# A norm's factor applied behind the matmul, with the shift as two further columns, in the last up stage of a float32 network

## The chip, the cores and the metric

The kernel runs on one core of a Trainium2 chip. The metric is the device time of one execution in microseconds (us). Durations of single instructions are in us too, unless ns is written. TensorE (PE) has two levels of clock, 1.2 and 2.4 GHz; the profile gives the granted clock as a share of the higher one.

## The reference, cut to what matters

A network on 256 tokens of width 1024, all in float32: a short-convolution layer, a latent-attention layer, and then one block of a second model with gated linear attention (GLA) and a squared-relu MLP. The change is in the MLP of that last block:

```
def modulate(h, shift, scale):
    return h * (1 + scale) + shift
def sqrelu_mlp(h, w1, w2):
    return jnp.square(jax.nn.relu(h @ w1)) @ w2
h_lat = h_lat + mod_l[2] * o_lat
h_lat = h_lat + mod_l[5] * sqrelu_mlp(modulate(rmsnorm(h_lat, norm2_g[i]), mod_l[3], mod_l[4]),
                                      mlp_w1[i], mlp_w2[i])
return rmsnorm(h_lat, final_g)
```

rmsnorm divides each token by the root of the mean of its squares and multiplies by a gain. w1 is 1024 x 4096, w2 is 4096 x 1024. The vectors mod_l (scale, shift, gates) are products of a condition with a large matrix (here "ada").

## The kernel before, in words

Activations lie feature-major: a tile of 128 partitions holds 128 features, and its T = 256 columns are the tokens. h holds the 8 chunks (DC) of the stream. A matmul multiplies a 128 x 128 block of weights with such a chunk; every product is made of three float32r matmuls, hi x hi, lo x hi and hi x lo, where hi is the value in float32r and lo the rest, so that the result has float32's precision.

The weights come as one stream of units: a unit is 128 x 1024, eight blocks, 24 matmuls. SyncE loads each position of the stream into a ring of four slots (raw). ScalarE makes whi by a copy (hi(), line 745), VectorE makes wlo by a subtraction (lo(), line 1154) and so frees the slot. TensorE starts a unit when its wlo is done (slot_of_next_unit). Both splits run three units ahead of TensorE (LEAD = 3); hi() of a unit waits until TensorE has finished the unit four before. Now and then a position holds a piece of the ada matrix instead; VectorE multiplies it with the condition (ada_dot, line 1236). Each engine has a program of its own, written out by hand in the order in which it runs; an engine waits at a semaphore, and everything behind that wait in its program waits too. Class Counts keeps the semaphores' counts: take waits for one more, sig raises, again waits for all counted so far.

The last block's end, for all engines:

- gla_out (8 units, inside resid(1, None, gate=2 * DC) on VectorE and resid(1, None) on ScalarE): when a unit's result is there, VectorE adds it, times the gate, to h (line 1322), ScalarE squares h (line 754), VectorE adds the square to ssum (line 1172) and makes the next wlo.
- The norm: TensorE's stat() sums ssum over the partitions (line 454, one plain float32 matmul that the trace shows as two), ScalarE takes the root (line 760), VectorE the reciprocal (line 1181, rstd). modulated then makes for each of the 8 chunks a32 = h x gmod x rstd on VectorE (line 1514), xhi = a32 + shift on ScalarE (line 930), and xlo on VectorE (line 1518).
- mlp_up, MC = 32 units, one result tile of 4096 features' 128 each: units(MC, DC, xhi, xlo, chunks=x_ready). The first two units are done together, chunk by chunk, as the chunks come (lines 390 to 392), the others one after the other (lines 408 to 410). For result j ScalarE makes mr = relu(result) (line 1121), VectorE ms = mr x mr (line 1689), ScalarE mhi of chunk j-1 (inner_hi, line 1116), VectorE mlo of chunk j-1 (inner_lo, line 1684) and then the next wlo. Chunks go in cycles of four: chunk 0 of a cycle has no inner part; at chunk 3 the inner part is done for 2 and for 3, and an ada product stands at the end. It is a loop of two times sixteen chunks.
- mlp_down, 8 results of four units each, which TensorE starts when 31 of the 32 mlo are there; then the last norm and the store.

The two up stages of the earlier layers (ffn_up) already have the norm's factor on the result: line 1260 multiplies the result by rstd on VectorE, line 785 is the step of ScalarE that follows.

Of the kernel before, what the change touches and what calls it, by code (L numbers as in the profile page):

```python
# [23 lines left out]
P = 128  # L24
T = 256
# [130 lines left out]
def at(t, k):  # L156

    return t[:, k * T:(k + 1) * T] if isinstance(k, int) else t[:, bass.ds(k * T, T)]


def program(nc, stream, xT, ctxT, vec, cst, rot, wa2, crow, out):
    ctx = ExitStack()

    def sb(name, cols, dt=F32, stack=ctx, rows=P):
        return stack.enter_context(nc.sbuf_tensor(name, [rows, cols], dt))

    with ctx:
# [96 lines left out]
        stage = ExitStack()  # L264
        mhi = sb("mhi", MC * T, F32R, stage)
        mlo = sb("mlo", MC * T, F32R, stage)
        mr = sb("mr", 4 * T, F32, stage)
        ms = sb("ms", 4 * T, F32, stage)
        stage.close()
        ps = [ctx.enter_context(nc.psum_tensor(f"ps{i}", [P, 512], F32)) for i in range(8)]  # L270
        STAT = ps[4]
# [40 lines left out]
        def cst_of(name):  # L312
            return ct[:, CST[name][0]:CST[name][0] + CST[name][1]]
# [2 lines left out]
            return rt_tab[:, ROT[name][0]:ROT[name][0] + ROT[name][1]]  # L316

        ones, ident = cst_of("ones"), cst_of("ident")
        ada_junk, cr_ctx = state[:, 0:D], state[:, D:2 * D]
        block = ctx.enter_context(nc.Block())  # L320

# [35 lines left out]
        def _(pe):  # L357
# [15 lines left out]
                c.n["unit"] = u + 1  # L373
                return u % RING

            def units(n, K, hi, lo, sizes=(BLK,), lag=RING, chunks=None, then=None, after=0, final=None):

                blk, begin = 0, 0  # L380
                if chunks is not None and then is None:
                    pair = [slot_of_next_unit() for _ in range(2)]
                    for j in range(2):
                        tile_free(tile[0] + j, lag)
                    for k in range(K):
                        c.take(chunks)
                        for j, slot in enumerate(pair):
                            dst = ps[(tile[0] + j) % lag][:, 0:T]
                            w = slice(slot * D + k * P, slot * D + (k + 1) * P)
                            pe.matmul(dst, whi[:, w], at(hi, k), start=(k == 0), stop=False)  # L390
                            pe.matmul(dst, whi[:, w], at(lo, k), start=False, stop=False)
                            last = pe.matmul(dst, wlo[:, w], at(hi, k), start=False, stop=(k == K - 1))
                            if k == K - 1:
                                c.sig(last, pe_units)
                    blk, begin = 2 * K, 2
                for j in range(begin, n):
                    slot = slot_of_next_unit()
                    for b in range(sizes[j % len(sizes)]):
                        t, k = tile[0] + blk // K, blk % K
                        if k == 0:  # L400
                            tile_free(t, lag)
                        dst = ps[t % lag][:, 0:T]
                        w = slice(slot * D + b * P, slot * D + (b + 1) * P)
                        if chunks is not None and j == 0 and begin == 0:
                            c.take(chunks)
                        if final is not None and k == K - 1:
                            pe.wait_ge(y_ready, final)
                        pe.matmul(dst, whi[:, w], at(hi, k), start=(k == 0), stop=False)  # L408
                        pe.matmul(dst, whi[:, w], at(lo, k), start=False, stop=False)  # L409
                        last = pe.matmul(dst, wlo[:, w], at(hi, k), start=False, stop=(k == K - 1))  # L410
                        blk += 1
                    c.sig(last, pe_units)
                    if then is not None and j == after:
                        then()
                tile[0] += blk // K
# [41 lines left out]
            def stat():  # L457
                c.take(ssum_ready, 8)
                stat_of([ssum[:, 0:T]])
# [250 lines left out]
            gla_stat(3)  # L710
            gla_out_chunks(4, DC)
            units(DC - 2, DC, zhi, zlo)
            stat()
            units(MC, DC, xhi, xlo, chunks=x_ready)
            c.take(y_ready, MC - 1)
            c.n["y_ready"] += 1
            looped(DC // 2, 8, MC, mhi, mlo, lag=2, final=c.n["y_ready"])
# [3 lines left out]
        def _(act):  # L721
            c = Counts(act)

            def settled():


                act.wait_ge(ev("tables"), 32)
# [70 lines left out]
            def resid(units_per, gain, gained=None, beside_ctx=False):  # L798


                per = {hi_ready: 4 * units_per, tile_read: 4, sq_ready: 8 if gained else 4}
                if gain:
                    per[xhi_ready] = 4
                if beside_ctx:
                    per |= {ev("zc_raw"): 4, ev("zc_hi"): 4}
                with c.loop(2, per) as i:
                    for m in range(4):
                        hi(units_per)
                        if beside_ctx:
                            settled()  # L810
                            c.take(ev("zc_raw"))
                            c.sig(act.activation(at(zhi, i * 4 + m), at(c32, i * 4 + m), ACT.Identity,
                                                 bias=mod[:, bass.ds(i * 4 + (6 * DC + m), 1)]), ev("zc_hi"))
                        settled()
                        c.take(tile_read)
                        if gain:
                            c.sig(act.activation(at(xhi, i * 4 + m), at(h, i * 4 + m), ACT.Copy,
                                                 scale=vt[:, bass.ds(i * 4 + (VEC[gain][0] + m), 1)]), xhi_ready)
                        square(h, i * 4 + m, 0 if gained else m)
                        if gained:  # L820
                            square(h, i * 4 + m, 1, vt_col(i * 4 + (VEC[gained][0] + m)))
# [105 lines left out]
            def modulated(dst, s0, units_after=()):  # L927
                for k in range(DC):
                    c.take(a_ready)
                    c.sig(act.activation(at(dst, k), at(a32, k), ACT.Identity, bias=mod[:, s0 + k:s0 + k + 1]), xhi_ready)  # L930
                    if k in units_after:
                        hi()
# [172 lines left out]
            head_hi(2)  # L1105
            head_root()
            head_hi(3)
            resid(1, None)
            sqrt_stat(D)
            modulated(xhi, 3 * DC)  # L1110
            c.n["pe_units"] = UNITS - 2 * MC
            with c.loop(2, {hi_ready: 16, pe_units: 16, tile_read: 16, y_f32: 16, yhi_ready: 16}) as i:
                def inner_hi(j):
                    settled()
                    c.take(y_f32)
                    c.sig(act.activation(at(mhi, i * 16 + j), at(ms, j % 4), ACT.Copy), yhi_ready)

                for j in range(16):
                    hi()
                    c.take(pe_units)  # L1120
                    c.sig(act.activation(at(mr, j % 4), ps[j % 4][:, 0:T], ACT.Relu), tile_read)
                    if j % 4:
                        inner_hi(j - 1)
                    if j % 4 == 3:
                        inner_hi(j)
# [13 lines left out]
        def _(dve):  # L1139
# [39 lines left out]
            def reciprocal_root(dst):  # L1179
                c.take(root_ready)  # L1180
                c.sig(dve.reciprocal(dst[:, :], root[:, :]), rstd_ready)  # L1181
                c.again(rstd_ready)
# [491 lines left out]
                head_norm(hd)  # L1674
            c.again(slots_done)
            mod_of(2 * DC, 5 * DC, 1, 4 * DC, "g_n2")
            resid(1, None, gate=2 * DC)
            reciprocal_root(rstd)
            modulated(h, DC, 3 * DC, xlo)
            with c.loop(2, {hi_ready: 16, "unit": 16, slots_done: 20, tile_read: 16, y_f32: 16, yhi_ready: 16,  # L1680
                            y_ready: 16}) as i:
                def inner_lo(j):
                    c.take(yhi_ready)
                    c.sig(dve.tensor_tensor(at(mlo, i * 16 + j), at(ms, j % 4), at(mhi, i * 16 + j), ALU.subtract),  # L1684
                          y_ready)

                for j in range(16):
                    c.take(tile_read)
                    c.sig(dve.tensor_tensor(at(ms, j % 4), at(mr, j % 4), at(mr, j % 4), ALU.mult), y_f32)
                    if j % 4:  # L1690
                        inner_lo(j - 1)
                    lo()
                    if j % 4 == 3:
                        inner_lo(j)
                        ada_dot(5 * DC + j // 4, i * 4 + (5 * DC + j // 4))
            c.again(slots_done)
            mod_of(5 * DC, 6 * DC, 0, 0, None)
            c.n["pe_units"] += MC
            clear_sum()

            def mlp_down(first):
# [132 lines left out]
```

## Time and profile before

| | us |
|---|---|
| median of 3 runs | 1019.96 |
| lowest and highest | 1016.63, 1024.02 |
| the profiled execution, its own time | 1022.39 |
| span of its profile | 1020.5 |
| granted clock of TensorE, mean | 0.986 |

The span runs from the first to the last instruction on the core. A timeline's or a chain's row gives the start, the duration, the engine (PEld is TensorE's weight load, an engine with q its sequencer), the line of the kernel, what is written and read, the count, and in brackets how long the engine stood idle before and who released it. ps is a result in PSUM.

### The profile page before, as it was taken

What the parts mean: (1) busy time and instruction counts of PE and PEld (TensorE: products, weight loads), DVE (VectorE), ACT (ScalarE), POOL (GpSimd) and SP (SyncE); (2) the same over time, 40 slices, a digit from 0 to 9 for tenths busy, and PEclk for the clock granted to TensorE, in tenths of its full rate; (3) what the DMA queues carried; (4) which work ended last, traced back from release to release, by engine and by line L of the source; (5) the groups of instructions that cost most, each with busy time, mean ns of one, the idle gap of its engine ahead of it and who ended that gap; (6) DMA issues with size and microseconds to landing.
All of it is one profiled execution on the core that took longest, in us unless ns stands there. A gap on an engine that the chain in (4) does not pass through costs nothing.

```text
span 1020.5 us, 21669 instructions
## 1 busy us (share of the span) xinstructions
PE 953.1 (93%) x7410; PEld 925.3 (91%) x7410; DVE 811.5 (80%) x1347; ACT 551.2 (54%) x876; POOL 1.2 (0%) x6
## 2 busy tenths in 40 slices
PE   4999999999999987999999997989999879999996
PEld 4999999999999877999999996878898879999995
DVE  5998899998889888899998887877536787775553
ACT  6545666665546435666666555766433456563331
POOL 0000000000000000000000000000000000000000
PEclk9999999999999999999999998999999989999998
DMA  8677565556786543555555884786530337766541
GB/s 328 216 247 242 167 203 185 185 185 198 271 267 223 173 148 103 177 195 191 184 185 177 288 263 141 240 287 209 185 103 22 124 121 243 235 226 207 184 165 41
DMA packets 54452, 197.32 MB, mean 193 GB/s; under 512 B 6046, under 2 KB 7198, under 8 KB 54144
## 3 DMA queue, kind: packets, MB, share of 16 engines
q1 hardware_dynamic: 54256, 195.55, 57.8%
q10 hardware_dynamic: 144, 1.05, 0.3%
q8 instruction: 36, 0.59, 0.2%
q14 instruction: 16, 0.13, 0.0%
HBM read 195.53 MB, written 1.05 MB: 193 GB/s over the span
## 4 chain that ended last, share of the span: by engine, by line
PE 80%; DVE 11%; ACT 3%; DMA 3%; issue 2%; DVEq 0%; SPq 0%; ACTq 0%
PE ps L408 23%; PE ps L410 23%; PE ps L409 23%; DVE wlo L1154 3%; DMA raw<-stream 2%; DVE raw L1236 1%; ACT whi L745 1%; PE ps L454 1%; PE ps L438 1%; DVE rstd L1181 1%; PE ps L440 1%; PE ps L439 1%; PE ps L574 1%; PE ps L590 1%; DMA ct<-cst 1%
## 5 line engine op out<-in xcount | busy, mean ns | idle before, releaser
L1154 DVE TENSOR_TENSOR wlo<-raw,whi 128x1024 fp32r<-128x1024 f32 x306 | 371.4, 1219 | 84.8 <-ACT whi L745 84.1
L745 ACT ACTIVATE whi<-raw 128x1024 fp32r<-128x1024 f32 x306 | 321.1, 1052 | 126.1 <-PE ps L410 60.2
L408 PE MATMUL ps<-xhi,whi 128*128 128x256 f32 x1288 | 366.3, 284 | 18.2 <-DVE wlo L1154 15.7
L409 PE MATMUL ps<-xlo,whi 128*128 128x256 f32 x1288 | 363.4, 282 | 0.0
L410 PE MATMUL ps<-xhi,wlo 128*128 128x256 f32 x1288 | 363.3, 282 | 0.0
L408 PEld LDWEIGHTS ps<-xhi,whi 128*128 128x128 f32 x1288 | 244.9, 190 | 19.7 <-issue 14.9
L409 PEld LDWEIGHTS ps<-xlo,whi 128*128 128x128 f32 x1288 | 245.0, 190 | 0.7 <-issue 0.5
L410 PEld LDWEIGHTS ps<-xhi,wlo 128*128 128x128 f32 x1288 | 245.0, 190 | 0.0
L408 PE MATMUL ps<-yhi,whi 128*128 128x256 f32 x400 | 112.5, 281 | 3.0 <-DVE ylo L1252 3.0
L409 PE MATMUL ps<-ylo,whi 128*128 128x256 f32 x400 | 112.3, 281 | 0.0
L410 PE MATMUL ps<-yhi,wlo 128*128 128x256 f32 x400 | 112.3, 281 | 0.0
L785 ACT ACTIVATE cv<-U,vt 128x256 f32<-128x256 f32 x88 | 44.9, 510 | 86.6 <-DVE U L1260 86.6
L408 PEld LDWEIGHTS ps<-yhi,whi 128*128 128x128 f32 x400 | 75.4, 189 | 3.4 <-issue 3.4
L409 PEld LDWEIGHTS ps<-ylo,whi 128*128 128x128 f32 x400 | 75.5, 189 | 0.0
L410 PEld LDWEIGHTS ps<-yhi,wlo 128*128 128x128 f32 x400 | 75.5, 189 | 0.0
L408 PE MATMUL ps<-mhi,whi 128*128 128x256 f32 x256 | 72.1, 282 | 2.5 <-DVE mlo L1684 1.6
L410 PE MATMUL ps<-mhi,wlo 128*128 128x256 f32 x256 | 71.9, 281 | 0.0
L409 PE MATMUL ps<-mlo,whi 128*128 128x256 f32 x256 | 71.9, 281 | 0.0
L1236 DVE SCALAR_TENSOR_TENSOR raw<-raw,cr 128x1024 f32<-128x1024 f32 x48 | 58.4, 1218 | 0.0
L408 PEld LDWEIGHTS ps<-mhi,whi 128*128 128x128 f32 x256 | 48.3, 189 | 2.9 <-issue 1.8
L409 PEld LDWEIGHTS ps<-mlo,whi 128*128 128x128 f32 x256 | 48.3, 189 | 0.0
L410 PEld LDWEIGHTS ps<-mhi,wlo 128*128 128x128 f32 x256 | 48.3, 189 | 0.0
(272 smaller groups left out, 1450.8 us busy)
## 6 DMA issues: line engine op xcount, KB each, us to landing
raw<-stream SPq DMA_DIRECT2D x362, 512.0 KB, 3.6
h<-xT SPq DMA_DIRECT2D x1, 1024.0 KB, 4.7
c<-ctxT ACTq DMA_DIRECT2D x1, 1024.0 KB, 7.1
out<-h SPq DMA_DIRECT2D x8, 128.0 KB, 2.1
ct<-cst SPq DMA_DIRECT2D x1, 962.5 KB, 6.8
rt_tab<-rot SPq DMA_DIRECT2D x1, 960.0 KB
cr<-crow SPq DMA_DIRECT2D x1, 512.0 KB, 10.6
state<-crow SPq DMA_DIRECT2D x1, 512.0 KB, 11.5
```

The source lines that it names most:

```text
L408: pe.matmul(dst, whi[:, w], at(hi, k), start=(k == 0), stop=False)
L409: pe.matmul(dst, whi[:, w], at(lo, k), start=False, stop=False)
L410: last = pe.matmul(dst, wlo[:, w], at(hi, k), start=False, stop=(k == K - 1))
L438: pe.matmul(dst, hi[:, tok], whi[:, w], start=first, stop=False)
L439: pe.matmul(dst, lo[:, tok], whi[:, w], start=False, stop=False)
L440: last = pe.matmul(dst, hi[:, tok], wlo[:, w], start=False, stop=final)
L454: last = pe.matmul(STAT[:, 0:width], ones, piece, start=(k == 0), stop=(k == len(pieces) - 1))
L574: pe.matmul(ps[5 + n % 3][:, b * T:(b + 1) * T], gates, sums[:, b * P:(b + 2) * P], start=True, stop=True)
L745: c.sig(act.activation(whi[:, s * D:(s + 1) * D], raw[:, r * D:(r + 1) * D], ACT.Copy), hi_ready)
L785: c.sig(act.activation(at(cv, j), U[:, j * (T + 2) + 2:(j + 1) * (T + 2)], ACT.Copy, scale=vt_col(i * 12 + (base + 3 * j + 2))), tap_ready)
L1154: c.sig(dve.tensor_tensor(wlo[:, w], raw[:, r], whi[:, w], ALU.subtract), slots_done)
L1236: c.sig(dve.scalar_tensor_tensor(out=tile_w, in0=tile_w, scalar=1.0, in1=cr[:, :], op0=ALU.mult, op1=ALU.mult, accum_out=into(t)), slots_done)
```

## The change

The normalised input of the last up stage is no longer made. In its place nhi and nlo hold h x gmod (no factor of the token), with chunks of T + 2 columns; the two further columns of each chunk hold the shift. As the factor is the same for all features of a token it is applied behind the matmul: each result, now 258 wide, is multiplied on VectorE by rstd2, which is rstd in 256 columns and 1 in the last two. So columns 0 to 255 hold the scaled part, and column 256 the shift's share, a number for each feature, which ScalarE's relu takes as its bias. ScalarE then squares too. The statistic stands behind the first unit of the stage (then=stat) and not ahead of it; TensorE waits for shift_ready before the stage. On ScalarE nhi is made inside the loop of gla_out, on VectorE nlo.

```diff
+def at2(t, k):
+    return t[:, k * (T + 2):(k + 1) * (T + 2)]
...
+        shift_twice = mod[:, 3 * DC:4 * DC].unsqueeze(2).to_broadcast([P, DC, 2])
+        def behind(t):
+            return t[:, :].rearrange("p (k t) -> p k t", t=T + 2)[:, :, T:T + 2]
...
@@ TensorE
-            stat()
-            units(MC, DC, xhi, xlo, chunks=x_ready)
+            pe.wait_ge(ev("shift_ready"), 2)
+            units(MC, DC, nhi, nlo, chunks=x_ready, then=stat, width=T + 2)
@@ ScalarE
-            resid(1, None)
+            with c.loop(2, {hi_ready: 4, tile_read: 4, sq_ready: 4, xhi_ready: 4}) as i:
+                for m in range(4):
+                    hi()
+                    settled()
+                    c.take(tile_read)
+                    c.sig(act.activation(nhi[:, bass.ds(i * (4 * (T + 2)) + m * (T + 2), T)], at(h, i * 4 + m), ACT.Copy,
+                                         scale=gmod[:, bass.ds(i * 4 + (DC + m), 1)]), xhi_ready)
+                    square(h, i * 4 + m, m)
+            act.activation(behind(nhi), shift_twice, ACT.Copy).then_inc(ev("shift_hi"), 1)
             sqrt_stat(D)
-            modulated(xhi, 3 * DC)
...
                 def inner_hi(j):
+                    c.again(y_f32)
                     settled()
-                    c.take(y_f32)
                     c.sig(act.activation(at(mhi, i * 16 + j), at(ms, j % 4), ACT.Copy), yhi_ready)
 
                 for j in range(16):
                     hi()
-                    c.take(pe_units)
-                    c.sig(act.activation(at(mr, j % 4), ps[j % 4][:, 0:T], ACT.Relu), tile_read)
+                    settled()
+                    c.take(tile_read)
+                    c.sig(act.activation(at(ms, j % 4), at2(mr, j % 4)[:, 0:T], ACT.Relu,
+                                         bias=at2(mr, j % 4)[:, T:T + 1]), ev("rectified"))
+                    c.again(ev("rectified"))
+                    c.sig(act.activation(at(ms, j % 4), at(ms, j % 4), ACT.Square), y_f32)
                     if j % 4:
                         inner_hi(j - 1)
@@ VectorE
-            resid(1, None, gate=2 * DC)
-            reciprocal_root(rstd)
-            modulated(h, DC, 3 * DC, xlo)
+            clear_sum()
+            with c.loop(2, {...}) as i:
+                def finish(m):
+                    c.take(xhi_ready)
+                    part = bass.ds(i * (4 * (T + 2)) + m * (T + 2), T)
+                    c.sig(dve.scalar_tensor_tensor(out=nlo[:, part], in0=at(h, i * 4 + m),
+                                                   scalar=gmod[:, bass.ds(i * 4 + (DC + m), 1)], in1=nhi[:, part],
+                                                   op0=ALU.mult, op1=ALU.subtract), x_ready)
+                    add_square(m)
+
+                for m in range(4):
+                    r, hm = result(1), at(h, i * 4 + m)
+                    c.sig(dve.scalar_tensor_tensor(out=hm, in0=r, scalar=mod[:, bass.ds(i * 4 + (2 * DC + m), 1)], in1=hm,
+                                                   op0=ALU.mult, op1=ALU.add), tile_read)
+                    if m:
+                        finish(m - 1)
+                    if m == 3:
+                        finish(3)
+                    lo()
+            dve.wait_ge(ev("shift_hi"), 1)
+            dve.tensor_tensor(behind(nlo), shift_twice, behind(nhi), ALU.subtract).then_inc(ev("shift_ready"), 2)
+            link(dve.memset(rstd2[:, T:T + 2], 1.0))
+            reciprocal_root(rstd2[:, 0:T])
...
                 for j in range(16):
-                    c.take(tile_read)
-                    c.sig(dve.tensor_tensor(at(ms, j % 4), at(mr, j % 4), at(mr, j % 4), ALU.mult), y_f32)
+                    c.sig(dve.tensor_tensor(at2(mr, j % 4), result(1, T + 2), rstd2[:, :], ALU.mult), tile_read)
                     if j % 4:
                         inner_lo(j - 1)
                     lo()
```

In units() the argument width, 256 by default, sets the columns of the result and of the chunks; the three matmuls are the same otherwise.

## Rows read from the trace of the kernel before

**Rows 1.** The page, TensorE: busy us, share of the span, instructions.

```profile
PE 953.1 (93%) x7410; PEld 925.3 (91%) x7410; DVE 811.5 (80%) x1347; ACT 551.2 (54%) x876; POOL 1.2 (0%) x6
```

**Rows 2.** The chain that ended last, around the start of mlp_up.

```profile
816.31 0.13 PE ps L410
816.68 0.49 DVE h L1322
817.42 0.42 ACT sq L754
817.87 0.44 DVE ssum L1172
818.35 0.71 PE ps L454 x2
819.15 0.39 ACT root L760
819.56 1.76 DVE rstd L1181
...
823.17 0.55 PE ps L390
```

**Rows 3.** Windows: length, busy us (count) of PE, PEld, DVE, ACT, POOL; clock, DMA.

```profile
375.00:395.00 20.00, 14.88 (x89) 12.46 (x87) 19.55 (x60) 9.53 (x35) 0.00 (x0) 1.00 0.50 162
...
823.20:827.60 4.40, 4.40 (x21) 4.40 (x22) 4.40 (x12) 3.01 (x6) 0.00 (x0) 0.50 0.00 0
...
828.00:917.00 89.00, 87.54 (x747) 87.34 (x745) 68.53 (x109) 53.62 (x97) 0.00 (x0) 1.00 0.68 221
...
839.41:850.67 11.26, 11.26 (x98) 11.26 (x98) 8.92 (x15) 7.62 (x13) 0.00 (x0) 1.00 0.75 243
```

**Rows 4.** Timeline of VectorE, within a cycle of mlp_up.

```profile
846.38 1.22 DVE L1154 TENSOR_TENSOR wlo<-raw,whi 128x1024 fp32r<-128x1024 f32 x1
848.42 0.42 DVE L1689 TENSOR_TENSOR ms<-mr 128x256 f32<-128x256 f32 x1 [0.82 <-ACT mr L1121]
848.86 0.42 DVE L1684 TENSOR_TENSOR mlo<-ms,mhi 128x256 f32 x1
849.20 1.22 DVE L1154 TENSOR_TENSOR wlo<-raw,whi 128x1024 fp32r<-128x1024 f32 x1
850.33 0.42 DVE L1684 TENSOR_TENSOR mlo<-ms,mhi 128x256 f32 x1
850.67 1.22 DVE L1236 SCALAR_TENSOR_TENSOR raw<-raw,cr 128x1024 f32<-128x1024 f32 x1
...
851.82 0.42 DVE L1689 TENSOR_TENSOR ms<-mr 128x256 f32<-128x256 f32 x1
```

**Rows 5.** Timeline of ScalarE, the same stretch.

```profile
848.00 0.38 ACT L1121 ACTIVATE mr<-ps 128x256 f32<-128x256 f32 x1 [1.18 <-PE ps L410]
848.28 0.41 ACT L1116 ACTIVATE mhi<-ms 128x256 f32 x1
848.98 0.42 ACT L1116 ACTIVATE mhi<-ms 128x256 f32 x1 [0.28 <-DVE ms L1689]
...
851.77 1.06 ACT L745 ACTIVATE whi<-raw 128x1024 fp32r<-128x1024 f32 x1 [0.57 <-DMA raw<-stream]
```

**Rows 6.** Lines 930 and 1260: ns min/median/max, first and last start us.

```profile
L930 ACT ACTIVATE xhi<-a,mod x16: 492/508/511, 626.9 to 826.6; 128x256 fp32r<-128x256 f32 x16
...
L1260 DVE TENSOR_TENSOR U<-ps,rstd x88: 414/424/425, 118.9 to 548.9; 128x256 f32<-128x256 f32 x88
```

**Rows 7.** Timeline, a handoff from VectorE to ScalarE in an earlier up stage.

```profile
430.09 0.42 DVE L1260 TENSOR_TENSOR U<-ps,rstd 128x256 f32<-128x256 f32 x1
...
430.60 0.51 ACT L785 ACTIVATE cv<-U,vt 128x256 f32<-128x256 f32 x1 [1.52 <-DVE U L1260]
```

**Rows 8.** The chain that ended last, the end of mlp_up and the start of mlp_down.

```profile
916.43 0.43 DVE mlo L1684
...
917.19 0.38 PE ps L408
```

More of the change, by code:

```diff
@@ L266, in program @@
         mlo = sb("mlo", MC * T, F32R, stage)
-        mr = sb("mr", 4 * T, F32, stage)
+        mr = sb("mr", 4 * (T + 2), F32, stage)
+        rstd2 = sb("rstd2", T + 2, F32, stage)
         ms = sb("ms", 4 * T, F32, stage)
+        nhi = sb("nhi", DC * (T + 2), F32R, stage)
+        nlo = sb("nlo", DC * (T + 2), F32R, stage)
         stage.close()
@@ L374, in slot_of_next_unit, with units @@
                 return u % RING
-            def units(n, K, hi, lo, sizes=(BLK,), lag=RING, chunks=None, then=None, after=0, final=None):
+            def units(n, K, hi, lo, sizes=(BLK,), lag=RING, chunks=None, then=None, after=0, final=None, width=T):
+                chunk = at if width == T else at2
                 blk, begin = 0, 0
@@ L401, in units @@
                             tile_free(t, lag)
-                        dst = ps[t % lag][:, 0:T]
+                        dst = ps[t % lag][:, 0:width]
                         w = slice(slot * D + b * P, slot * D + (b + 1) * P)
@@ L407, in units @@
                             pe.wait_ge(y_ready, final)
-                        pe.matmul(dst, whi[:, w], at(hi, k), start=(k == 0), stop=False)
-                        pe.matmul(dst, whi[:, w], at(lo, k), start=False, stop=False)
-                        last = pe.matmul(dst, wlo[:, w], at(hi, k), start=False, stop=(k == K - 1))
+                        pe.matmul(dst, whi[:, w], chunk(hi, k), start=(k == 0), stop=False)
+                        pe.matmul(dst, whi[:, w], chunk(lo, k), start=False, stop=False)
+                        last = pe.matmul(dst, wlo[:, w], chunk(hi, k), start=False, stop=(k == K - 1))
                         blk += 1
@@ L1107, in _ @@
             head_hi(3)
-            resid(1, None)
+            with c.loop(2, {hi_ready: 4, tile_read: 4, sq_ready: 4, xhi_ready: 4}) as i:
[7 more added lines that the diff above has]
+            act.activation(behind(nhi), shift_twice, ACT.Copy).then_inc(ev("shift_hi"), 1)
             sqrt_stat(D)
-            modulated(xhi, 3 * DC)
             c.n["pe_units"] = UNITS - 2 * MC
-            with c.loop(2, {hi_ready: 16, pe_units: 16, tile_read: 16, y_f32: 16, yhi_ready: 16}) as i:
+            with c.loop(2, {hi_ready: 16, tile_read: 16, ev("rectified"): 16, y_f32: 16, yhi_ready: 16}) as i:
                 def inner_hi(j):
+                    c.again(y_f32)
                     settled()
-                    c.take(y_f32)
                     c.sig(act.activation(at(mhi, i * 16 + j), at(ms, j % 4), ACT.Copy), yhi_ready)
@@ L1676, in _ @@
             mod_of(2 * DC, 5 * DC, 1, 4 * DC, "g_n2")
-            resid(1, None, gate=2 * DC)
-            reciprocal_root(rstd)
-            modulated(h, DC, 3 * DC, xlo)
-            with c.loop(2, {hi_ready: 16, "unit": 16, slots_done: 20, tile_read: 16, y_f32: 16, yhi_ready: 16,
+            clear_sum()
+            with c.loop(2, {hi_ready: 4, "unit": 4, slots_done: 4, pe_units: 4, tile_read: 4, sq_ready: 4, ssum_ready: 4,
+                            xhi_ready: 4, x_ready: 4}) as i:
+                def finish(m):
[18 more added lines that the diff above has]
+            reciprocal_root(rstd2[:, 0:T])
+            c.n["pe_units"] = PHASE_AT["mlp_up"]
+            with c.loop(2, {hi_ready: 16, "unit": 16, slots_done: 20, pe_units: 16, tile_read: 16, yhi_ready: 16,
                             y_ready: 16}) as i:
@@ L1697, in _ @@
             mod_of(5 * DC, 6 * DC, 0, 0, None)
-            c.n["pe_units"] += MC
             clear_sum()
```

## The prediction

> **What bounds the kernel now.** I read the page first: TensorE is busy for 93% of the span [rows 1], so a change can gain only where TensorE waits, and can lose wherever it makes TensorE wait. Then the chain that ended last, around the boundary before the last up stage [rows 2]. The last result of gla_out is finished at about 816.4 us and the first matmul of the up stage (L390) starts at 823.17: 6.8 us in which the chain runs through h, its square, the sum, the statistic on TensorE, the root, a reciprocal of 1.76 us and the normalised chunk. The windows [rows 3] show two things more. From 823.20 to 827.60 TensorE does 21 matmuls where 4.4 us at full clock would hold 4.4 / 0.117 = 38: the granted clock is 0.50, the 1.2 GHz level, and that costs about 2 us. And from 828 to 917 it is at 1.00, busy 87.5 of 89 us: here the matmuls bind. One cycle of four chunks takes 839.41 to 850.67 = 11.26 us, 96 matmuls of 0.117 us. VectorE is busy 8.9 us of it and ScalarE 7.6; each has slack, but VectorE also makes wlo, without which TensorE has no next unit.
>
> Last the timelines of VectorE and ScalarE in that cycle [rows 4, 5]. The reader is to see that nothing in it is a round trip that VectorE sits out. The relu is ScalarE's, straight from PSUM; VectorE squares; and mhi of the chunk before (848.28) is issued right behind the relu (848.00), so it is there before VectorE asks for it at 848.86. The wlo follows at 849.20.
>
> **The change part by part.**
>
> *Boundary.* Removed ahead of the first matmul: statistic, root, reciprocal, and the first normalised chunk. New: the PE waits for the shift columns, which stand behind the whole split. Step by step from [rows 2]: h(7) starts at 816.68; ScalarE's nhi(7) where the square started, 817.42, with a per-partition factor 0.51 us [rows 6], to 817.93; nlo(7) on VectorE 817.96, sum 0.40 later at 818.36, wlo 818.70, and 1.14 later (849.20 to 850.33 [rows 4]) the small subtraction for the columns at 819.84, about 0.2 us. The first matmul starts at 820.1, 3.1 us earlier than now. The gap is then 3.7 us in place of 6.8. Whether the clock still falls the trace does not show: full 0.117 or half 0.21 for the first unit, so 2.8 or 5.1 us. I take the full clock, since the gap is nearly halved, and keep 2.3 us (with the statistic at half clock 3 us) for the upper end.
> The statistic now stands behind unit 0, at 822.9. From there to the end of the reciprocal it is 818.35 to 821.32 = 3.0 us [rows 2], so VectorE can rescale result 0 (call this moment M0) at 825.9. Meanwhile TensorE does units 1 and 2, whose wlo is there. This costs nothing on TensorE but the statistic, at most 0.7 us. Within gla_out's loop VectorE gets one more 0.40 us instruction per chunk and ScalarE one of 0.41, beside a unit of 2.8 us: hidden, also if a handoff of 0.3 is added.
>
> *Width.* 258 columns for 256 make 24 x 0.117 x 2/256 = 0.02 us a unit, 0.7 in all if TensorE binds, nothing where it waits.
>
> *Loop of the up stage.* This decides. Per chunk VectorE now multiplies the result by rstd2 (M), ScalarE then does relu with the bias column, waits for its own relu, squares, waits for its own square (the wait of inner_hi is for all squares counted so far, this chunk's included), and only then converts chunk j-1 to mhi. VectorE, in order, stands before inner_lo(j-1) until that mhi is done, and the wlo of the next unit is queued behind it. So each chunk has one whole round trip VectorE, ScalarE, VectorE, in series with the 1.14 us of wlo. Terms:
> mult 0.42 (as L1260, result times rstd [rows 6]); handoff 0.10 (U ends 430.51, cv starts 430.60 [rows 7]); relu with a bias column 0.51 (L930 [rows 6]); own wait; square 0.41; own wait; mhi 0.41 [rows 5]; handoff back; mlo to wlo 0.34 and wlo 1.14 [rows 4]. The trace shows no ScalarE instruction waiting for its own predecessor. Bounds by the nearest rows: 0.03 (sum after square, 817.84 to 817.87) and 0.26 (square after h, 817.16 to 817.42 [rows 2]). In between lies 0.14 (ms ends 848.84, mhi starts 848.98 [rows 4, 5]). I take 0.06 for the first, whose operands are fixed, 0.10 for the second and 0.10 for the way back.
> Sum: 0.42 + 0.10 + 0.51 + 0.06 + 0.41 + 0.10 + 0.41 + 0.10 + 0.34 + 1.14 = 3.6 us for chunks 1 and 2 of a cycle. Chunk 3 has a second mlo and the ada product behind it, 850.33 to 851.82 = 1.5 more: 5.1. Chunk 0 has no inner part: 0.34 + 1.14 = 1.5; but its relu and square put ScalarE's next whi (0.96) in the way of relu 1, which starts 2.4 after M0 in place of 2.0, so chunks 0 and 1 together take 5.4. Cycle: 5.4 + 3.6 + 5.1 = 14.1 us against 11.26 now. TensorE needs 11.35 and will wait for wlo, 2.8 us in each cycle. The ring of three units ahead evens out the short and the long chunks, no more.
> The landing of raw does not add: the whi at 851.77 waited for data whose slot was freed by the wlo that ended at 847.60, 4.2 us [rows 4, 5]; with 14.1 us for five positions that lies earlier than each use.
>
> *End of the stage.* From M28, seven cycles after M0, to M31 it is 5.4 + 3.6 = 9.0; from M31 the round trip to mlo(30) is 2.1, mlo 0.42, and 0.34 until TensorE starts (mlo from 916.43 [rows 8]). Mlp_down starts at 825.9 + 7 x 14.1 + 9.0 + 2.9 = 936.5 against 917.19 [rows 8]: 19.3 later. Behind that nothing changes: the next wlo, at M31 + 7.1, is needed at about M31 + 11.
>
> The profiled execution took 1022.39 us, 1.9 more than its span of 1020.5; with 19.3 it gives 1041.7. It is 2.4 above the median of the three runs, 1019.96, on which I forecast 1039.3; as the two waits of ScalarE on itself are more likely to be longer than shorter than what I took, I say 1040.
> Ends: with 0.03 at each handoff a chunk is 3.35 and the cycle 13.3: 825.9 + 93.4 + 8.5 + 2.6 = 930.4, +13.2. With 0.27 each and 0.20 for the way back a chunk is 4.24, the cycle 16.4, the end 825.9 + 114.5 + 10.6 + 3.5 = 954.5, +37.3, and +40 if the first unit is at half clock.
>
> **The clock, by rule and row.** The stretch 375 to 395 has TensorE at 14.9 of 20 us with waits in between, and the granted clock is 1.00 [rows 3]; the new stage would be at 11.35 of 14.1, so I take the full clock in it. The Trainium skill (Perfetto Trace Analysis, Matmul Optimizations) says that the engine scales with its utilization and that matmuls should be issued back to back; by it the waits in the loop could bring the clock down, which is rival B. The trace does not bear it out at this share.
>
> **Rivals.**
> A. TensorE still binds and only the boundary counts (not slower). If chunk j's chain ran beside wlo, VectorE's eight short instructions at 0.34, four wlo and the ada product, 2.7 + 4.6 + 1.2 = 8.5 in 11.35, would fit. Decides below 2.8 us a chunk on average. For it: busy shares leave room. Against: the queues are in order and the wait names this chunk's square. Time: -3.1 (start) - 2.1 (half clock) + 0.7 (statistic) + 0.7 (width) = -3.8: 1016.
> B. The clock falls to 1.2 GHz in the waits and stays. 96 matmuls x 0.21 = 20.2 a cycle, TensorE binds: 8 x (20.2 - 11.26) = +72 less the 3 at the start: 1089. For: it fell once, after 6.8 us of waiting. Against: [rows 3].
> C. 258 columns leave the fast form of the matmul. One plain f32 product of 256 columns (two passes, L454) took 0.71 us [rows 2]; already at twice 0.117 a unit is 5.6 and the cycle 22.5: 1019.96 + 90 - 3 = 1107. Against: 2 columns more change no type.
> D. The round trip binds but overlaps in part (mlo waits less than I count), cycle 11.8 to 12.8: -3 + 8 x 1.0 = about +5: 1025.
>
> **How the numbers follow.** Forecast 0.82, A 0.04, B 0.05, C 0.03, D 0.06. Predicted 1040. The range goes from 1031 (low end 1033 and 2 us of spread between runs) to 1058 (median plus 37.3); B, C, most of A and D lie outside, under 2 in 10. One per cent, 10 us, is about what a measurement of this kernel can tell from no change. Faster by over 1%: 0.01. Within 1%: A and most of D, 0.09. Slower: 0.90.
>
> **What would show it.** Right: mlp_down's first matmul near 936; VectorE's costliest wait in the stage is for mhi, ahead of mlo; TensorE waits for wlo, about 2.8 us a cycle; four chunks every 14.1 us; first matmul of the stage at 820; ScalarE's relu 0.51. Wrong: the cycle at 11.35 with VectorE waiting for TensorE (A), a granted clock of 0.5 in the stage (B), matmul starts over 0.2 apart at full clock (C).

## The result, and the profile after

| | before | changed |
|---|---|---|
| median, us (6 runs each) | 1020.3 | 1045.79 |
| lowest and highest | 1016.63, 1024.02 | 1043.24, 1047.62 |
| span of the profile | 1020.5 | 1042.7 |
| granted clock, mean | 0.986 | 0.979 |
| one cycle of four chunks in mlp_up | 11.26 | 14.08 |
| first matmul of mlp_up | 823.17 | 819.66 |
| first matmul of mlp_down | 917.19 | 937.75 |

The changed kernel is slower: ratio 1.0225, 95% interval 1.0203 to 1.0247, which is 21 to 25 us. (The two medians divided give 1.025, just above that interval.) Line numbers shift by 10 to 50: L408 to L410 are now L420 to L422, wlo is L1177, the multiplication by rstd2 L1733, relu L1141, ScalarE's square L1144, mhi L1135, mlo L1729.

The page's row of busy time, to be read against [rows 1]:

```profile
PE 964.0 (92%) x7410; PEld 931.5 (89%) x7410; DVE 807.0 (77%) x1341; ACT 567.9 (54%) x909; POOL 1.2 (0%) x6
```

VectorE has 4.5 us less to do, ScalarE 17 us more, and both have the same share of the span or less than before. No engine became full. What binds shows in the waits of 826 to 943 (total us, times, longest):

```profile
DVE mlo L1729 <- ACT mhi L1135: 43.5, 24, 2.0
ACT ms L1141 <- DVE mr L1733: 36.0, 24, 2.3
PEld ps L420 <- DVE wlo L1177: 15.1, 20, 1.0
PE ps L420 <- DVE wlo L1177: 11.0, 20, 0.8
...
PE ps L420 <- DVE mlo L1729: 7.1, 1, 7.1
```

VectorE waits 24 times for mhi (all chunks but the first of each cycle: 3 x 8), ScalarE 24 times for VectorE's product. Two engines that wait for one another in turn are a round trip. TensorE waits for wlo 20 times. No wait for a DMA stands in the whole list, so late weights are not what holds the stage. Here is one chunk of it, first VectorE's timeline, then ScalarE's; in [rows 4] VectorE had no wait for ScalarE's conversion:

```profile
846.81 0.42 DVE L1733 TENSOR_TENSOR mr<-ps,rstd 128x258 f32<-128x258 f32 x1
848.93 0.42 DVE L1729 TENSOR_TENSOR mlo<-ms,mhi 128x256 f32 x1 [1.70 <-ACT mhi L1135]
849.27 1.22 DVE L1177 TENSOR_TENSOR wlo<-raw,whi 128x1024 fp32r<-128x1024 f32 x1
850.41 0.42 DVE L1733 TENSOR_TENSOR mr<-ps,rstd 128x258 f32<-128x258 f32 x1
```

```profile
847.27 0.51 ACT L1141 ACTIVATE ms<-mr 128x256 f32<-128x256 f32 x1 [1.15 <-DVE mr L1733]
847.81 0.42 ACT L1144 ACTIVATE ms<-ms 128x256 f32<-128x256 f32 x1
848.35 0.42 ACT L1135 ACTIVATE mhi<-ms 128x256 f32 x1
```

From product to product 850.41 - 846.81 = 3.60 us, and a unit of 24 matmuls is over in 2.87. The boundary, from the chain that ended last, against [rows 2]:

```profile
816.07 0.49 DVE h L1713
816.80 0.52 ACT nhi L1125
818.30 1.22 DVE wlo L1177
824.32 0.45 PE ps L466 x2
825.33 1.77 DVE rstd L1204
827.30 0.44 DVE mr L1733
```

And windows of the changed kernel (columns as in [rows 3]):

```profile
819.70:823.00 3.30, 3.30 (x19) 3.30 (x20) 0.00 (x0) 0.00 (x0) 0.00 (x0) 0.66 0.54 160
...
841.30:855.40 14.10, 12.38 (x98) 11.74 (x98) 8.67 (x15) 8.96 (x16) 0.00 (x0) 1.00 0.59 187
...
937.75:943.66 5.91, 5.91 (x27) 5.91 (x28) 4.16 (x7) 0.72 (x2) 0.00 (x0) 0.50 0.61 189
```

In the stage the clock is granted in full in spite of its waits. Around the stage it falls to half in two places: from about a microsecond behind the first matmul at 819.66, which had waited 3.85 us, and from 937.75 on, after a wait of 7.1 us.

### The profile page after: what moved, and what is told of

Same layout as the page of the kernel before. It is cut to its first block, busy times and chain, and to the rows that moved or that the text cites. A ratio compares the mean times of both kernels' runs of the same rounds, so it can differ in the third digit from the quotient of the medians.

```text
span 1042.7 us, 21761 instructions
## 1 busy us (share of the span) xinstructions
PE 964.0 (92%) x7410; PEld 931.5 (89%) x7410; DVE 807.0 (77%) x1341; ACT 567.9 (54%) x909; POOL 1.2 (0%) x6
## 4 chain that ended last, share of the span: by engine, by line
PE 72%; DVE 15%; ACT 6%; issue 3%; DMA 2%; DVEq 1%; ACTq 0%; SPq 0%
PE ps L420 21%; PE ps L421 20%; PE ps L422 20%; DVE wlo L1177 5%; DVE raw L1259 2%; ACT ms L1141 2%; ACT whi L757 2%; DMA raw<-stream 1%; PE ps L466 1%; ACT ms L1144 1%; PE ps L450 1%; DVE rstd L1204 1%; ACT mhi L1135 1%; PE ps L452 1%; PE ps L451 1%
## 5 line engine op out<-in xcount | busy, mean ns | idle before, releaser
L1177 DVE TENSOR_TENSOR wlo<-raw,whi 128x1024 fp32r<-128x1024 f32 x306 | 372.1, 1221 | 86.5 <-ACT whi L757 85.6
L420 PE MATMUL ps<-xhi,whi 128*128 128x256 f32 x1048 | 299.0, 285 | 18.3 <-DVE wlo L1177 15.7
L421 PE MATMUL ps<-xlo,whi 128*128 128x256 f32 x1048 | 296.1, 282 | 0.0
L422 PE MATMUL ps<-xhi,wlo 128*128 128x256 f32 x1048 | 296.0, 282 | 0.0
L420 PEld LDWEIGHTS ps<-xhi,whi 128*128 128x128 f32 x1048 | 199.7, 191 | 19.7 <-issue 14.9
L421 PEld LDWEIGHTS ps<-xlo,whi 128*128 128x128 f32 x1048 | 199.8, 191 | 0.7 <-issue 0.5
L422 PEld LDWEIGHTS ps<-xhi,wlo 128*128 128x128 f32 x1048 | 199.7, 191 | 0.0
L420 PE MATMUL ps<-yhi,whi 128*128 128x256 f32 x400 | 112.3, 281 | 3.0 <-DVE ylo L1275 3.0
L422 PE MATMUL ps<-yhi,wlo 128*128 128x256 f32 x400 | 112.1, 280 | 0.0
L420 PE MATMUL ps<-nhi,whi 128*128 128x258 f32 x256 | 75.9, 297 | 14.9 <-DVE wlo L1177 11.0
L420 PE MATMUL ps<-mhi,whi 128*128 128x256 f32 x256 | 73.1, 286 | 8.0 <-DVE mlo L1729 7.1
L420 PEld LDWEIGHTS ps<-yhi,whi 128*128 128x128 f32 x400 | 75.3, 188 | 3.4 <-issue 3.4
L422 PEld LDWEIGHTS ps<-yhi,wlo 128*128 128x128 f32 x400 | 75.3, 188 | 0.0
L421 PE MATMUL ps<-nlo,whi 128*128 128x258 f32 x256 | 72.9, 285 | 0.0
L422 PE MATMUL ps<-mhi,wlo 128*128 128x256 f32 x256 | 72.8, 284 | 0.0
L422 PE MATMUL ps<-nhi,wlo 128*128 128x258 f32 x256 | 72.7, 284 | 0.0
L420 PEld LDWEIGHTS ps<-nhi,whi 128*128 128x128 f32 x256 | 48.9, 191 | 19.4 <-DVE wlo L1177 15.1
```

The lines of the kernel that those rows point to most:

```text
L420: pe.matmul(dst, whi[:, w], chunk(hi, k), start=(k == 0), stop=False)
L421: pe.matmul(dst, whi[:, w], chunk(lo, k), start=False, stop=False)
L422: last = pe.matmul(dst, wlo[:, w], chunk(hi, k), start=False, stop=(k == K - 1))
L1177: c.sig(dve.tensor_tensor(wlo[:, w], raw[:, r], whi[:, w], ALU.subtract), slots_done)
```

## The experiments

Theory T: the new order puts a round trip VectorE, ScalarE, VectorE in series with the next wlo. Rivals: S, the load ScalarE got; W, the width of 258. Eight kernels were run on chips, each beside the kernel before. The kernel before took 1023.41 us (median) beside e1 to e4 and 1022.76 beside e5 to e8, in place of 1020.3, so a time is compared across these groups by its ratio and not by its median. The earlier stages of the profiled runs differ by up to 4.5 us; to take that out, the table counts from the start of the last h of gla_out (h(7), L1322 before). "Ahead of mlp_down" is TensorE's wait there.

| kernel | ratio to before (95%) | cycle, us | first matmul | mlp_down starts | TensorE's wait ahead of mlp_down |
|---|---|---|---|---|---|
| before | 1 | 11.26 | +6.49 | +100.5 | 1.6 |
| changed | 1.0225 (1.0203 to 1.0247) | 14.08 | +3.59 | +121.7 | 7.1 |
| e1 wlo first | 0.9995 (0.9975 to 1.0015) | 11.46 | +3.59 | +100.5 | 2.9 |
| e2 mhi first | 0.9975 (0.9955 to 0.9995) | 11.47 | +3.59 | +98.5 | 1.1 |
| e3 one more instruction | 1.0364 (1.0312 to 1.0415) | 15.92 | +3.60 | +136.4 | 8.9 |
| e4 square on VectorE | 1.0133 (1.0085 to 1.0182) | 12.66 | +3.60 | +110.4 | 4.7 |
| e5 narrow wait | 1.0136 (1.0109 to 1.0164) | 13.37 | +3.60 | +116.0 | 6.4 |
| e6 shift early | 0.9931 (0.9909 to 0.9953) | 11.47 | no wait | +93.1 | 1.1 |
| e7 both orders | 0.9942 (0.9923 to 0.9962) | 11.47 | no wait | +94.2 | 2.3 |
| e8 width 256 | 0.9916 (0.9889 to 0.9942) | 11.44 | no wait | +92.9 | 1.1 |

**e1: the next wlo ahead of the inner part (VectorE).**

```diff
+                    lo()
                     if j % 4:
                         inner_lo(j - 1)
-                    lo()
                     if j % 4 == 3:
```

> One line moved on VectorE: the next wlo is made directly behind the multiplication by rstd2, ahead of the wait for mhi; no instruction is added or dropped. Theory T (wlo stands in series behind the round trip VectorE, ScalarE, VectorE): the chain runs beside wlo, TensorE binds again, a cycle of four chunks goes from 14.08 us to 11.3 to 11.5, mlp_down starts near 914 in place of 937.75, the time is 1015 to 1020. Theory S (the load that ScalarE got, relu with a bias column and the square, is what costs) and theory W (the 258 wide matmuls cost): nothing of that is changed by the order, so the cycle stays above 13 us and the time above 1038.

Measured: ratio 0.9995, cycle 863.45 to 874.91 = 11.46 us. The whole loss of the stage is gone by moving one line, with every instruction kept. S and W are out as causes of the loss: load and width are those of the changed kernel. VectorE still waits for mhi 24 times, but the waits now stand behind wlo and sum to little, in the same stage's waits (826 to 950):

```profile
DVE mlo L1729 <- ACT mhi L1135: 11.0, 24, 0.6
```

The ratio is at the slow end of what T expected, and mlp_down starts at +100.5 where "near 914" would be about +98; why is taken up below.

**e2: mhi of the chunk before, ahead of the wait for this chunk (ScalarE).**

```diff
                     hi()
+                    if j % 4:
+                        inner_hi(j - 1)
                     settled()
                     c.take(tile_read)
...
                     c.sig(act.activation(at(ms, j % 4), at(ms, j % 4), ACT.Square), y_f32)
-                    if j % 4:
-                        inner_hi(j - 1)
```

> The same round trip cut at its other end: ScalarE converts chunk j-1 to mhi ahead of its wait for the product of chunk j, and VectorE's order stays as in the changed kernel. T: mhi(j-1) is there before VectorE asks for it, cycle 11.3 to 11.5 us, time 1014 to 1019; a little under the kernel with wlo moved, as the last chunks' mlo come 1 to 2 us sooner and TensorE's gap ahead of mlp_down shrinks from 7.4 us to under 2. S and W: unchanged against the changed kernel, above 1038.

Measured: 0.9975, cycle 861.51 to 872.98 = 11.47. The chain cut at the other end gives the same cycle, and the stage's end is 2.0 us earlier than in e1, of which 1.8 is TensorE's shorter wait ahead of mlp_down. VectorE's timeline has its old form again, mlo and wlo right behind the product, and the wait is for TensorE:

```profile
869.37 0.43 DVE L1733 TENSOR_TENSOR mr<-ps,rstd 128x258 f32<-128x258 f32 x1 [0.97 <-PE ps L422]
869.71 0.42 DVE L1729 TENSOR_TENSOR mlo<-ms,mhi 128x256 f32 x1
870.04 1.22 DVE L1177 TENSOR_TENSOR wlo<-raw,whi 128x1024 fp32r<-128x1024 f32 x1
```

**e3: the chain made longer.** A copy of the square onto itself on ScalarE; the result is unchanged by it.

```diff
-                    c.sig(act.activation(at(ms, j % 4), at(ms, j % 4), ACT.Square), y_f32)
+                    c.sig(act.activation(at(ms, j % 4), at(ms, j % 4), ACT.Square), ev("rectified"))
+                    c.again(ev("rectified"))
+                    c.sig(act.activation(at(ms, j % 4), at(ms, j % 4), ACT.Copy), y_f32)
```

> The suspected chain made longer: a third ScalarE instruction per chunk (a copy of the square onto itself, with a wait for its predecessor) between the square and mhi; the result is the same. T: every chunk with an inner part is longer by the copy and one more own wait, 0.42 + 0.03 to 0.12 = 0.45 to 0.54 us, and chunk 1 also by the copy in front of its relu; a cycle grows by 1.8 to 2.1 us to 15.9 to 16.2, the time by 14 to 17 to 1060 to 1063. If a slack in ScalarE or TensorE took it up (TensorE binding, W), the time would stay within 2 us of the changed kernel's 1045.8.

Measured: 1.0364, cycle 859.91 to 875.83 = 15.92. Against the changed kernel it is 14.1 us more in the traces from h(7) to the end (240.7 against 226.6) and 1.4% by the ratios, the low end of the 14 to 17 expected. (The median, 1060.04, stands beside a kernel before that was 3 us slower in that group.) A chunk with an inner part, product to product, is 4.06:

```profile
866.22 0.42 DVE L1735 TENSOR_TENSOR mr<-ps,rstd 128x258 f32<-128x258 f32 x1
868.80 0.43 DVE L1731 TENSOR_TENSOR mlo<-ms,mhi 128x256 f32 x1 [2.16 <-ACT mhi L1135]
869.15 1.22 DVE L1179 TENSOR_TENSOR wlo<-raw,whi 128x1024 fp32r<-128x1024 f32 x1
870.28 0.42 DVE L1735 TENSOR_TENSOR mr<-ps,rstd 128x258 f32<-128x258 f32 x1
```

0.46 more a chunk for an instruction of 0.42: ScalarE's time counts in full here, although it is busy for only 55% of the span. That is what a chain does and a load does not.

**e4: the square back on VectorE**, all else as changed.

```diff
-                    c.sig(act.activation(at(ms, j % 4), at2(mr, j % 4)[:, 0:T], ACT.Relu,
+                    c.sig(act.activation(at2(mr, j % 4)[:, 0:T], at2(mr, j % 4)[:, 0:T], ACT.Relu,
                                          bias=at2(mr, j % 4)[:, T:T + 1]), ev("rectified"))
-                    c.again(ev("rectified"))
-                    c.sig(act.activation(at(ms, j % 4), at(ms, j % 4), ACT.Square), y_f32)
...
                     c.sig(dve.tensor_tensor(at2(mr, j % 4), result(1, T + 2), rstd2[:, :], ALU.mult), tile_read)
+                    c.take(ev("rectified"))
+                    r = at2(mr, j % 4)[:, 0:T]
+                    c.sig(dve.tensor_tensor(at(ms, j % 4), r, r, ALU.mult), y_f32)
```

> The square goes back to VectorE (as in the kernel before), the rest of the change stays: norm factor behind the matmul, shift as bias, 258 columns. T: VectorE now waits for relu only, and mhi of the chunk before runs beside the square: mult 0.42, handoff 0.04, relu 0.51, back 0.03 to 0.16, square to mlo 0.34 to 0.5, mlo 0.34, wlo 1.14, together 2.9 to 3.0 a chunk, 4.4 for the fourth, 2.5 for the first: cycle 12.7 to 12.9 us, time 1034 to 1037. S: ScalarE loses its square, the whole loss goes, about 1018. W: no change, 1045.

Measured: 1.0133, cycle 855.79 to 868.45 = 12.66, just under the 12.7 to 12.9 expected. So the square's place explains a part, and not because of ScalarE's load: with the square gone from it, the shorter round trip product, relu, square is still in front of wlo:

```profile
864.07 0.42 DVE L1731 TENSOR_TENSOR mr<-ps,rstd 128x258 f32<-128x258 f32 x1
865.07 0.43 DVE L1734 TENSOR_TENSOR ms<-mr 128x256 f32<-128x256 f32 x1 [0.58 <-ACT mr L1141]
865.50 0.42 DVE L1727 TENSOR_TENSOR mlo<-ms,mhi 128x256 f32 x1
865.84 1.22 DVE L1175 TENSOR_TENSOR wlo<-raw,whi 128x1024 fp32r<-128x1024 f32 x1
```

Chunks of 2.9 us look harmless beside units of 2.87; it is the fourth, with the ada product, that makes 12.66 out of it.

**e5: the wait of mhi narrowed** to the square it reads.

```diff
-                def inner_hi(j):
-                    c.again(y_f32)
+                def inner_hi(j, back=0):
+                    c.again(y_f32, back)
...
                     if j % 4:
-                        inner_hi(j - 1)
+                        inner_hi(j - 1, 1)
```

> The chain made shorter: the conversion of chunk j-1 to mhi waits for the squares up to chunk j-1 only, not for the square of chunk j in front of it. It can then start 0.31 behind the square's start in place of 0.54: a chunk goes from 3.60 to 3.37 us, four chunks in a cycle from 14.08 to 13.2 to 13.4 (chunk 0 has no inner part, but chunk 1 does), the time falls by 5 to 7 against the changed kernel, to a ratio of 1.015 to 1.018 against the kernel before. If the own wait is hidden behind something else: 1.0225 as before it.

Measured: 1.0136, cycle 857.70 to 871.07 = 13.37 (counted from chunk 1 to chunk 1), a chunk 3.36 to 3.37. In the traces, from h(7) to the end of the span, it is 220.3 against 226.6: 6.3 us, within the 5 to 7 expected; the ratios differ by 9 us, with intervals that allow 4 to 14. The ratio itself is a little under the 1.015 to 1.018 expected, with an interval that reaches into it. ScalarE's rows show where the 0.23 comes from: mhi starts 0.32 behind the square, before the square's row has ended, where in the changed kernel it starts 0.54 behind it.

```profile
862.39 0.42 ACT L1144 ACTIVATE ms<-ms 128x256 f32<-128x256 f32 x1
862.71 0.40 ACT L1135 ACTIVATE mhi<-ms 128x256 f32 x1
```

A wait that asks for more than is read costs its time in every chunk once it lies in the chain.

**e6: the shift columns ahead of gla_out's loop**, on top of e2.

```diff
+            act.wait_ge(ev("shift_there"), 1)
+            act.activation(behind(nhi), shift_twice, ACT.Copy).then_inc(ev("shift_hi"), 1)
             with c.loop(2, {hi_ready: 4, tile_read: 4, sq_ready: 4, xhi_ready: 4}) as i:
...
-            act.activation(behind(nhi), shift_twice, ACT.Copy).then_inc(ev("shift_hi"), 1)
...
             mod_of(2 * DC, 5 * DC, 1, 4 * DC, "g_n2")
+            dve.memset(rstd2[:, T:T + 2], 1.0).then_inc(ev("shift_there"), 1)
             clear_sum()
+            dve.wait_ge(ev("shift_hi"), 1)
+            dve.tensor_tensor(behind(nlo), shift_twice, behind(nhi), ALU.subtract).then_inc(ev("shift_ready"), 2)
```

(The same lines behind the loop are dropped, and reciprocal_root waits for shift_there.)

> On top of the kernel with mhi first: the shift columns of nhi and nlo are written before the loop of gla_out, so that TensorE's wait for them is over long before the stage. The first matmul of the up stage follows the last of gla_out and the stage waits only for chunk 7 (h, nhi, nlo: about 1.8 us), in place of 3.3 us for everything; the gap stays under 2 us, so the clock stays at 1.00 in unit 0 where 12 matmuls ran at half speed. Gain 1.5 to 3.4 for the wait, 1.2 for the clock: 3 to 5 us under the kernel with mhi first, ratio 0.992 to 0.995 against the kernel before. Rival: the two small instructions in front of the loop delay gla_out by as much: ratio 0.9975.

Measured: 0.9931, interval 0.9909 to 0.9953, the lowest ratio of the complete versions: 5 to 9 us under the kernel before and 2.9% under the changed one. TensorE's timeline goes from gla_out to mlp_up without a break, and the window shows the clock in full:

```profile
816.02 0.28 PE L421 MATMUL ps<-zlo,whi 128*128 128x256 f32 x1
816.14 0.28 PE L422 MATMUL ps<-zhi,wlo 128*128 128x256 f32 x1
816.26 0.28 PE L420 MATMUL ps<-nhi,whi 128*128 128x258 f32 x1
```

```profile
815.50:821.00 5.50, 5.50 (x46) 5.45 (x45) 4.45 (x8) 2.74 (x5) 0.00 (x0) 1.00 0.38 133
```

I had expected a wait under 2 us for chunk 7. There is none, since chunks 0 to 6 are 21 matmuls, 2.5 us of work, and nlo(7) is there at 818.67, about 0.1 us before chunk 7's first matmul at 818.80: a narrow margin. Mlp_down starts 5.4 us earlier than in e2 (+93.1 against +98.5), a little more than the 3 to 5 expected.

**e7: e6 with e1's order too.**

> The kernel with early shift columns, with the next wlo moved ahead of the inner part on VectorE too. If TensorE alone binds in the stage, a second cut of the same chain gives nothing: within 0.2% of the kernel with early shift columns, or 1 to 2 us slower, since mlo of chunk 30 then stands behind a wlo at the stage's end (2.9 us of gap there in the kernel with wlo moved, 1.1 in the one with mhi first).

Measured: 0.9942; its interval and e6's overlap, the cycle is the same 11.47, and mlp_down starts 1.1 us later, where TensorE waits 2.3 in place of 1.1. Once TensorE binds, the second cut only puts a wlo in front of mlo(30) at the end.

**e8: e6 with all of it 256 wide.** Matmuls, product and result lose the two columns, and relu's bias is a fixed column of the modulation; the shift's share is left out of the result.

> Measures the two further columns alone, on the kernel with early shift columns: matmuls, multiplication and results 256 wide, relu's bias a fixed column of the modulation in place of the shift's product, so that the shift's share is left out of the result; instruction counts are the same. TensorE binds here, so the time shows the width: matmuls in the stage were 0.1194 us apart at 258 columns and 0.1173 or 0.1187 at 256. Expected 0.0007 to 0.0021 x 768 = 0.5 to 1.6 us less than with 258. Theory W (the width costs more than its share of columns) would show over 3 us.

Measured: 0.9916 against 0.9931, intervals overlapping; cycle 11.44 against 11.47, mlp_down 0.2 us earlier. The two columns cost 0.2 us in the stage, under the 0.5 to 1.6 expected, and the times cannot separate it. (From h(7) to the end e8 is 1.2 us shorter, but 1.0 of that lies in mlp_down, where the edit changes nothing.) W is out. But the cycle of 11.26 that the kernel before had at the same 256 columns did not come back. The chunks of nhi and nlo still stand 258 columns apart in e8; whether that placing matters was not run.

## Why the prediction was right, point by point

**The mechanism and its size: right.** The cycle was forecast at 14.1 and is 14.08; a chunk at 3.6 and is 3.60. The single terms were off by hundredths that cancel: first handoff 0.04 (847.27 less the product's end at 847.23) where I took 0.10; relu 0.51 as taken; own waits 0.03 and 0.12 where I took 0.06 and 0.10; square and mhi 0.42 each for 0.41; the way back 0.16 for 0.10. TensorE's loss by waiting was forecast at 2.8 a cycle: counted from start to start it is 14.08 less 96 x 0.1197 = 2.6, of which the window shows 1.7 as idle, because a matmul's row lasts 0.28 and so covers the first part of a wait. e3 and e5 move the chain by plus 0.46 and minus 0.23 a chunk, and cycle and time follow; e1 and e2 cut it and the loss is gone. That the chain is the cause is thereby shown, not argued.

**Chunk 0 and 1 together** were forecast at 5.4: from 841.41 to 846.81 it is 5.40.

**The boundary: the first matmul right, what follows it 2 us too early.** TensorE started 3.6 us after h(7), forecast 3.4. The step that failed is "I take the full clock, since the gap is nearly halved". The wait was not nearly halved. Inside the 6.8 us of the kernel before stands the statistic, 818.35 to 819.06 [rows 2], and the granted clock is still 1.00 there; it falls in the wait behind it (0.69 from 819.50 to 823.00). That wait was 4.1 us, up to 823.17, and the new one is 3.85. In the changed kernel the clock fell about a microsecond into unit 0, 15 of its 24 matmuls ran 0.214 apart, and unit 0 took 819.66 to 824.14 = 4.5 us for 2.8. The bound I kept for it (plus 2.3) covered it. The statistic to the product took 3.16, forecast 3.0. M0 came 11.2 us after h(7), forecast 9.2. Rival B's "it fell once, after 6.8 us of waiting" misreads the same rows.

**The end of the stage: its start of mlp_down right, a term missing behind it.** From M28 (925.88) to mlp_down (937.75) is 11.9, as forecast. "Behind that nothing changes" is the sentence that failed. TensorE had finished its last unit long before the round trips of chunks 29 to 31 were through, waited 7.1 us, and came back at half clock for 27 matmuls: 27 x (0.214 - 0.119) = 2.6 us. In the trace mlp_down to the end takes 104.95 for 103.31, so 1.0 of that was given back. The step of the matmuls was shorter in that run (0.1173 for 0.1187 apart, 768 of them: 1.1), which accounts for it. The prediction has no term for that, so this offset is luck.

**The sum.** Forecast +19.3, said as +20; the traces have +22.2, the medians +25.5, the ratio of runs 21 to 25. From h(7) to the end, where the 0.6 us by which h(7) came earlier in the changed kernel's trace is out, it is 226.6 - 203.8 = 22.8, so 3.5 over the forecast: 1.9 up to the start of mlp_down (1.7 of clock, the rest handoffs and the statistic) and 1.6 behind it (2.6 of clock less 1.0 given back). Both clock terms come from pricing TensorE's waits by their length: the first was left out of the forecast and kept for the upper end only, the second was in neither. The medians are further apart than the traces because the profiled execution of the kernel before was 2.1 us above its median and that of the changed kernel 0.3 below.

**Rivals.** A did not happen in the changed kernel but is what e1 and e2 are. Its time was forecast at 3.8 us below before; e2 is 0.5 to 4.6 below, and e1 2.6 below to 1.5 above. There the gains were given back: the clock fell after the first wait too, the matmuls stand 0.1194 apart where the kernel before had 0.1173 (768 x 0.0021 = 1.6), and e1 waits 1.3 longer ahead of mlp_down, with 14 matmuls at half clock behind it (14 x 0.095 = 1.3). Only e6, which takes the wait away, gets the gain and more. B did not come: the clock is 1.00 in the stage, with 20 waits of at most 0.8 us in it, and it is 1.00 in e3's cycle too, where TensorE waits up to 1.7 us. The advice of the Trainium skill (Perfetto Trace Analysis, Matmul Optimizations) to issue matmuls back to back agrees with the trace at the two long waits; at the 20 short ones the trace shows no price in the clock. C is refuted by the changed kernel's own matmuls, 258 wide and 0.1197 apart, and D by the cycle.

## What to carry to other kernels

Where two engines hand a tile to and fro, look at what stands in each queue behind a wait: what a third engine lives from (here the next wlo) belongs ahead of the wait, or what is waited for must come from the step before. Busy shares of 80% and 54% before (77% and 54% after) said there was room, and there was none; the sum from one product to the next said 3.6 us against the 2.8 of a unit before anything was built. And a long wait of the matmul engine can have two prices, its length and the half speed behind it.

## What was not expected of the hardware

- How much of a half-clock stretch follows a wait of TensorE in these traces, counted as matmuls that start 0.2 us or more before the next: none to one after 1.1, 1.6, 1.7 and 2.3 us, 14 after 2.9, 13 to 17 after the 3.85 at the start of the stage (five experiments and the changed kernel), 20 after the 4.1 of the kernel before, 27 after 4.7, 19 after 6.4, 27 after 7.1, but 17 after 8.9. Longer waits do not always cost more.
- At a granted clock of 1.00 the matmuls of one and the same stage stand at different distances in different runs: mlp_down's, all 256 wide, 0.1187 or 0.1173 us, mlp_up's 0.1173 in before and 0.1192 in e8 with the same width. That is 1 to 2% of a stage, 1.1 to 1.5 us for 768 matmuls. The width does not explain it. In mlp_down the five runs that came out of their wait at half clock (changed, e1, e3, e4, e5) all have 0.1173 afterwards; of the other five, before, e2, e6 and e7 have 0.1187, but e8 has 0.1173; what decides it stays open.
- Where ScalarE waits for its own predecessor, the next instruction starts 0.03 us behind the end of the one before if its operands are fixed (relu to square; in e3 also square to copy) and 0.12 or 0.13 behind it if they are addressed through the loop's register (square to mhi, in e3 copy to mhi). That the register makes the difference is not shown. And the gap is not all that the wait costs: in e5, without it, mhi starts before the square has ended, and a chunk is shorter by 0.23.
